# Two transformer blocks on one core: the meta columns moved behind the tokens in the rows of the second block's activations

## What is computed

```python
h = jnp.concatenate([meta, x], axis=1)                  # 16 + 256 rows
hn = rms_norm_2(h, norm_mix_g)
u, gb_in, gc_in, v_in, ga_lin, gbr_lin = jnp.split(hn @ w_in, splits, axis=-1)
pooled = causal_multiscale_pool(u)                       # trailing means over 2, 4, 8, 16 positions
y_a = jnp.einsum("blgc,gcd->blgd", pooled, pool_w) * pool_scale
y_b = (gb_in * causal_depthwise_conv(gc_in * v_in, conv_w)) @ conv_out_w     # 3 taps
h = h + (g_a * y_a + g_b * y_b) @ w_o
...
return rms_norm_2(h, norm_final_g)[:, N_META:]
```

## Time and profile before

| | us |
|---|---|
| median of 3 runs | 2633.67 (2633.49 to 2633.74) |
| the profiled execution | 2633.6 |
| its span in the trace | 2631.8 |
| PE busy | 2620.6 |
| PEld busy | 2558.4 |
| DVE busy | 1572.1 |
| ACT busy | 1172.8 |

### The profile page before, as it was taken

How to read it: one execution, slowest core, us unless ns; L and a number is a source line. 1 busy time by engine, 2 the same in 40 slices (tenths; PEclk the granted TensorE clock), 3 DMA queues, 4 the chain that set the end, 5 groups by cost and what they waited for, 6 DMA issues and landing times.

```text
span 2631.8 us, 50881 instructions
## 1 busy us (share of the span) xinstructions
PE 2620.6 (100%) x21394; PEld 2558.4 (97%) x21394; DVE 1572.1 (60%) x1557; ACT 1172.8 (45%) x1259; POOL 0.8 (0%) x7
## 2 busy tenths in 40 slices
PE   9999999999999999999999999999999999999998
PEld 8989999999999999999999999999999989998997
DVE  6567765555555556795676666556755555555555
ACT  5346544434443444465333333444454434443444
POOL 0000000000000000000000000000000000000000
PEclk9999999999999999999999999999999999999999
DMA  8654655555555565556555555555555555555553
GB/s 294 196 168 145 208 189 192 195 193 192 191 192 193 191 199 194 180 203 199 176 178 189 181 189 180 198 188 199 197 193 192 194 195 191 194 197 194 191 193 128
DMA packets 254275, 503.33 MB, mean 191 GB/s; under 512 B 8130, under 2 KB 11652, under 8 KB 253988
## 3 DMA queue, kind: packets, MB, share of 16 engines
q1 hardware_dynamic: 252180, 497.61, 57.4%
q10 hardware_dynamic: 1952, 3.68, 0.4%
HBM read 498.37 MB, written 2.88 MB: 190 GB/s over the span
## 4 chain that ended last, share of the span: by engine, by line
PE 99%; DMA 0%; DVE 0%; ACT 0%; SPq 0%; issue 0%; DVEq 0%; ACTq 0%
PE ps L1368 49%; PE ps L1379 24%; PE ps L1397 4%; PE ps L1399 4%; PE ps L1398 4%; PE ps L1417 4%; PE ps L1426 4%; PE ps L1421 4%; PE ps L1405 0%; PE ps L1406 0%; PE ps L1407 0%; DMA xtok<-in_x_dram 0%; PE ps L1562 0%; PE ps L1561 0%; PE ps L1560 0%; PE ps L1484 0%
## 5 line engine op out<-in xcount | busy, mean ns | idle before, releaser
L821 DVE TENSOR_TENSOR lo<-raw,hi 128x1024 fp32r<-128x1024 f32 x940 | 1144.5, 1224 | 920.6 <-ACT hi L494 905.7
L494 ACT ACTIVATE hi<-raw 128x1024 fp32r<-128x1024 f32 x940 | 991.6, 1060 | 1243.5 <-PE ps L1379 935.8
L1368 PE MATMUL ps<-A,hi 128*128 128x256 f32 x7283 | 903.6, 277 | 0.0
L1368 PEld LDWEIGHTS ps<-A,hi 128*128 128x128 f32 x7283 | 861.0, 188 | 0.3
L1368 PE MATMUL ps<-B,hi 128*128 128x256 f32 x3962 | 491.3, 277 | 0.0
L1379 PE MATMUL ps<-A,lo 128*128 128x256 f32 x3648 | 488.0, 276 | 0.0
L1368 PEld LDWEIGHTS ps<-B,hi 128*128 128x128 f32 x3962 | 468.1, 188 | 0.1
L1379 PEld LDWEIGHTS ps<-A,lo 128*128 128x128 f32 x3648 | 447.4, 188 | 0.0
L1379 PE MATMUL ps<-B,lo 128*128 128x256 f32 x1984 | 265.3, 276 | 0.0
L1379 PEld LDWEIGHTS ps<-B,lo 128*128 128x128 f32 x1984 | 243.2, 188 | 0.0
L1398 PE MATMUL ps<-lo,B 128*128 128x512 f32 x336 | 130.8, 389 | 0.0
(11 more groups left out here) (243 smaller groups left out, 1196.8 us busy)
## 6 DMA issues: line engine op xcount, KB each, us to landing
raw<-in_w_in_dram SPq DMA_DIRECT2D x136, 1024.0 KB, 5.1
raw<-in_ffn_w_dram SPq DMA_DIRECT2D x132, 1024.0 KB, 5.1
raw<-in_w_gate_up_dram SPq DMA_DIRECT2D x88, 1024.0 KB, 5.0
raw<-in_w_down_dram SPq DMA_DIRECT2D x44, 1024.0 KB, 5.0
raw<-in_w_out_dram SPq DMA_DIRECT2D x16, 1024.0 KB, 5.1
raw<-in_pl_w_gate_dram SPq DMA_DIRECT2D x16, 1024.0 KB, 5.1
raw<-in_conv_out_w_dram SPq DMA_DIRECT2D x16, 1024.0 KB, 5.0
raw<-in_w_o_dram SPq DMA_DIRECT2D x16, 1024.0 KB, 5.0
```

Of the source, the lines that this page charges most:

```text
L494: act.activation(hi[:, slot % RING], raw[:, raw_slot, 2 * (slot % 2):2 * (slot % 2) + 2, :], ACT.Copy).then_inc(hi_ready, 1)
L821: dve.tensor_tensor(lo[:, slot % RING], raw[:, slot // 2 % RAWS, 2 * (slot % 2):2 * (slot % 2) + 2, :], hi[:, slot % RING], ALU.subtract). ...
L1368: pe.matmul(ps[:, b0 + m, 0:T], high(slot, kk, m), x, start=j == 0 and kk == 0 and part == 0, stop=False)
```

## The change

The rows of B are laid out anew for the second block's mixer, and the products of with_meta take other column ranges. In a row of B the tokens' high parts now stand at columns 0 to 255, behind them the last two meta tokens' high parts (256, 257), their low parts (258, 259), the other fourteen's high parts (260 to 273) and low parts (274 to 287); the tokens' low parts stand at 320 to 575. One product of the high pass covers the tokens, the meta tokens' high parts and their low parts; the low-part pass covers the tokens alone; the third pass covers the tokens and the meta tokens' high parts.

```diff
-TOKEN_AT = META + 16
+TOKEN_AT = 16
+LOW_AT = 320
-LO_META = TM + T
+AHEAD_HI, AHEAD_LO, REST_HI, REST_LO = T, T + 2, T + 4, T + 4 + VT0
...
-        B_halves = B[:, :, META:META + 2 * T]
-        B_token = B[:, :, TOKEN_AT:TOKEN_AT + 2 * T]
+        B_high, B_low = B[:, :, 0:T], B[:, :, LOW_AT:LOW_AT + T]
...
                 elif step == "split_meta":
...
-                    given.mark(act.activation(B[:, :, 0:META], metaT[:, :, :], ACT.Copy))
+                    act.activation(B[:, :, AHEAD_HI:AHEAD_HI + 2], metaT[:, :, VT0:META], ACT.Copy)
+                    given.mark(act.activation(B[:, :, REST_HI:REST_HI + VT0], metaT[:, :, 0:VT0], ACT.Copy))
...
                 elif kind == "u2":
                     dve.wait_ge(pieces_used, end)
-                    dve.tensor_tensor(meta_low[:, :, VT0:META], ps[:, b0:b0 + 4, TM:TM + 2], row_of(r_row[:, VT0:META], MT), ALU.mult)
-                    dve.tensor_tensor(meta_low[:, :, 0:VT0], ps[:, b0:b0 + 4, TM + 2:TM + META], row_of(r_row[:, 0:VT0], MT), ALU.mult)
-                    dve.tensor_tensor(win_a[:, :, :], ps[:, b0:b0 + 4, 0:TM], row_of(r_row[:, :], MT), ALU.mult).then_inc(psum_free, 1)
+                    ahead_r, rest_r = row_of(r_row[:, VT0:META], MT), row_of(r_row[:, 0:VT0], MT)
+                    dve.tensor_tensor(meta_low[:, :, VT0:META], ps[:, b0:b0 + 4, AHEAD_LO:AHEAD_LO + 2], ahead_r, ALU.mult)
+                    dve.tensor_tensor(meta_low[:, :, 0:VT0], ps[:, b0:b0 + 4, REST_LO:REST_LO + VT0], rest_r, ALU.mult)
+                    dve.tensor_tensor(win_a[:, :, VT0:META], ps[:, b0:b0 + 4, AHEAD_HI:AHEAD_HI + 2], ahead_r, ALU.mult)
+                    dve.tensor_tensor(win_a[:, :, 0:VT0], ps[:, b0:b0 + 4, REST_HI:REST_HI + VT0], rest_r, ALU.mult)
+                    dve.tensor_tensor(win_a[:, :, META:TM], sums, Rm, ALU.mult).then_inc(psum_free, 1)
...
             def with_meta(seg, g, j, slot, b0, n):
-                ahead = META if seg.reads[1] == "wide" else META - VT0
+                with_lo, with_hi = (REST_LO + VT0, REST_LO) if seg.reads[1] == "wide" else (AHEAD_LO + 2, AHEAD_LO)
...
-                        pe.matmul(ps[:, b0 + m, 0:ahead + T], high(slot, kk, m), B[:, 2 * j + kk, META - ahead:TM],
+                        pe.matmul(ps[:, b0 + m, 0:with_lo], high(slot, kk, m), B[:, 2 * j + kk, 0:with_lo],
...
-                        pe.matmul(ps[:, b0 + m, ahead:ahead + T + ahead], high(slot, kk, m), B[:, 2 * j + kk, TM:TM + T + ahead],
+                        pe.matmul(ps[:, b0 + m, 0:T], high(slot, kk, m), B_low[:, 2 * j + kk, :],
...
-                        last = pe.matmul(ps[:, b0 + m, 0:ahead + T], low(slot, kk, m), B[:, 2 * j + kk, META - ahead:TM],
+                        last = pe.matmul(ps[:, b0 + m, 0:with_hi], low(slot, kk, m), B[:, 2 * j + kk, 0:with_hi],
```

More of the change, by code:

```diff
@@ L252, in bass_two_blocks @@
         ones = sb("ones", [P, P])
+        r_row = sb("r_row", [P, TM])
+        vec2 = sb("vec2", [P, V2N])
         vec1 = sb("vec1", [P, V1K])
@@ L508, in wait_group, with high_parts @@
                 act.nop(nofuse=True)
-            def high_parts(buf, k, a, src, name, n=MT):
+            def high_parts(to, k, src, name, n=MT):
                 for i in range(n):
-                    last = act.activation(buf[:, bass.ds(k + i, 1), a:a + T], src(i), ACT.Copy, scale=gain(name, k + i))
+                    last = act.activation(to[0][:, bass.ds(k + i, 1), :], src(i), ACT.Copy, scale=gain(name, k + i))
                 return last
@@ L563, in evacuate @@
                     more()
-                    given.mark(high_parts(A, k, 0, lambda i: some(h, k + i, 1, 0, T), "ffn" if kind == "res_ffn" else "ffn2"))
+                    given.mark(high_parts(A_parts, k, lambda i: some(h, k + i, 1, 0, T), "ffn" if kind == "res_ffn" else "ffn2"))
                     ready.skip()
@@ L574, in evacuate @@
                     wait_alone(asked)
-                    given.mark(act.activation(some(A if kind == "cb" else to_b, k, 4, 0, T), work[:, :, :], ACT.Copy))
+                    given.mark(act.activation(some((A_parts if kind == "cb" else to_b)[0], k, 4, 0, T), work[:, :, :], ACT.Copy))
                     ready.skip()
@@ L679, in side @@
                     wait(asked)
-                    given.mark(act.activation(some(B_halves, 8 + 4 * c, 4, 0, T), V8[:, 4 * c:4 * c + 4, :], ACT.Copy))
+                    given.mark(act.activation(some(B_high, 8 + 4 * c, 4, 0, T), V8[:, 4 * c:4 * c + 4, :], ACT.Copy))
                     ready.skip()
@@ L746, in side @@
                         for i in range(2):
-                            last = act.activation(B_halves[:, 2 * hd + i, 0:T], ps[:, 6, i * T:(i + 1) * T], ACT.Copy, scale=small[:, 20 + i:21 + i])
+                            last = act.activation(B_high[:, 2 * hd + i, :], ps[:, 6, i * T:(i + 1) * T], ACT.Copy, scale=small[:, 20 + i:21 + i])
                         given.mark(last)
@@ L833, in free_sums, with low_parts @@
                 dve.wait_ge(psum_free, G + 1)
-            def low_parts(buf, k, a, src, name, n=MT):
+            def low_parts(to, k, src, name, n=MT):
                 for i in range(n):
-                    last = dve.scalar_tensor_tensor(out=buf[:, bass.ds(k + i, 1), a + T:a + 2 * T],
-                                                    in0=src(i), scalar=gain(name, k + i), in1=buf[:, bass.ds(k + i, 1), a:a + T],
+                    last = dve.scalar_tensor_tensor(out=to[1][:, bass.ds(k + i, 1), :],
+                                                    in0=src(i), scalar=gain(name, k + i), in1=to[0][:, bass.ds(k + i, 1), :],
                                                     op0=ALU.mult, op1=ALU.subtract)
@@ L969, in evacuate @@
                     more()
[L970 removed]
+                    finish_split(A_parts, k)
                 elif kind == "pool":
@@ L1012, in times_gain, with finish_split @@
                 dve.tensor_tensor(x, x, row_of(gfin_row[:, bass.ds(gi * GC, GC)], 2), ALU.mult)
-            def finish_split(buf, k):
+            def finish_split(to, k):
                 given.skip()
                 wait(given)
-                ready.mark(dve.tensor_tensor(some(buf, k, 4, T, 2 * T), work[:, :, :], some(buf, k, 4, 0, T), ALU.subtract))
+                ready.mark(dve.tensor_tensor(some(to[1], k, 4, 0, T), work[:, :, :], some(to[0], k, 4, 0, T), ALU.subtract))
             def rsqrt(var, mid, r, src, scale, meanwhile=lambda: None):
@@ L1245, in side @@
                         for i in range(2):
-                            last = dve.scalar_tensor_tensor(out=B_halves[:, 2 * hd + i, T:2 * T], in0=ps[:, 6, i * T:(i + 1) * T],
-                                                            scalar=small[:, 20 + i:21 + i], in1=B_halves[:, 2 * hd + i, 0:T],
+                            last = dve.scalar_tensor_tensor(out=B_low[:, 2 * hd + i, :], in0=ps[:, 6, i * T:(i + 1) * T],
+                                                            scalar=small[:, 20 + i:21 + i], in1=B_high[:, 2 * hd + i, :],
                                                             op0=ALU.mult, op1=ALU.subtract)
@@ L1361, in highs @@
                     for part in range(2):
-                        x = X[:, k, at + part * T:at + (part + 1) * T]
+                        x = X[part][:, k, :]
                         for m in range(MT):
@@ L1557, in last_pieces @@
                             k = 2 * j + kk
-                            Xh, Xl = B_token[:, k, a * P:(a + 1) * P], B_token[:, k, T + a * P:T + (a + 1) * P]
+                            Xh, Xl = (x[:, k, a * P:(a + 1) * P] for x in token_parts)
                             to = ps[:, b0 + a, :]
```

41 lines of the change are left out of this document (21 added, 20 removed).

## The result

The changed kernel takes 2638.94 us (median of 18 runs, 2638.69 to 2639.54) where the kernel before takes 2633.76 (18 runs, 2633.49 to 2634.29): **5.2 us more**, a ratio of 1.002 with a 95% interval of 1.0012 to 1.0027. Not one run of the one overlaps one of the other. The forecast was 2631.3 us, the range 2626.5 to 2634.0.

The account below looks back on a forecast made before the run. The prediction took PE's back-to-back products to bound the kernel; gains of 2.1 and 2.6 us less costs of 0.4, 1.7 and 0.2 made -2.4 us against 2633.6, stated as 2631.3 us, range 2626.5 to 2634.0.

Parts of the forecast that it names:

- What bounds the kernel: Whole kernel: time is the sum of PE's product prices; PE is busy 2620.6 of 2631.8 us and waits three times.
- The passes: Convolution and pooled path: columns move between passes, no product added or removed; terms sum to -2.4 us.
- Convolution: Low-part pass 258 to 256 columns gains 2.1 us; high pass 258 to 260 costs 0.4 more; third pass unchanged.
- Pooled path: Low-part pass 272 to 256 gains 2.6 us; high pass to 288 costs 1.7, third pass to 274 costs 0.2.
- the rule of the Trainium skill: Isolated product spacing: columns over 2.4 GHz plus 2.5 ns; convolution would gain nothing, pooled path lose 0.2 us.
- The other engines: DVE's extra small instructions and ACT's split copy of the meta columns stay hidden; costed at nothing.
- Rival 4: Cut product behind the third pass leaves PE dear; some 3260 later 256s cost 4.5 ns more: 2646 us, chance 0.04.
- Rivals 1 and 3: 1: 256s between wide passes stay dear, 2633.8 us, chance 0.14; 3: third pass keeps the cheap state, 2626.6 us, 0.08.
- Rival 2: Wide passes: the 5.5 ns extra comes from operands' start places, so no product pays it afterwards: 2620.5 us, chance 0.08.

Follow-up runs that it names:

- e11: Changed kernel with r_row and vec2 between B and h, so h, ident, ones lie where they lay before and B stays as changed: 2630.63 us.
- e3: Changed kernel with r_row and vec2 put back between A and B: 2676.01 us.
- e4: Kernel before with only r_row and vec2 moved behind ones: 2684.13 us.
- e5: Kernel before with vec2 alone moved behind ones: 2665.05 us.
- e6: Changed kernel with vec2 alone put back between A and B: 2671.40 us.
- e7: Kernel before with rstd_meta (64 bytes) ahead of hi rather than behind lo: 2729.94 us.
- e8: Kernel before with rstd_meta ahead of hi and also r_row and vec2 moved behind ones: 2698.74 us.
- e12: Changed kernel with r_row and vec2 ahead of ident, so ident and ones lie where before but h stays moved: 2636.19 us.
- e13: Kernel before with ln_stats (96 bytes) moved to between B and h: 2639.10 us.
- e14: Kernel before with vec1 (328 bytes) moved to between B and h: 2639.13 us.
- e1: Changed kernel with one product cut in two in the piece behind each of three fp32 side steps: 2631.20 us.
- e15: Kernel before with double_rstd one piece earlier and the second turn of h one piece later, no address changed: 2633.75 us.
- e16: Changed kernel with double_rstd one piece earlier and the second turn of h one piece later, no address changed: 2639.01 us.
- e9: Changed kernel with cuts behind three fp32 side steps, placed one piece later (ga piece 8, f2_up0 pieces 5 and 13): 2631.24 us.
- e10: Kernel before with cuts at ga piece 8 and f2_up0 pieces 5 and 13: 2633.96 us.
- e2: Kernel before with one product cut in two at ga piece 7 and f2_up0 pieces 4 and 12: 2640.01 us.

## Why the prediction was wrong, point by point

**What bounds the kernel** was right: PE's products, one after another, no waits. The whole 5.6 us can be added up from the chain's pieces.

**The passes.** The sum of -2.4 us was mis-sized by little: -2.8 measured (e11 against the kernel before gives -3.1 in all). That it came so near is in part luck, for the two misses, 0.9 us too little gain in the convolution and 0.5 too much in the pooled path, are of opposite sign. By terms:
- Convolution, -2.1 + 0.4 = -1.7 forecast, -2.6 measured. The low-part pass stands at 0.92 where 0.93 was assumed, which makes -2.8 us where -2.1 was forecast; the high pass of 260 did not get dearer by 0.84 ns a product, it costs 0.96 like the 258; the third pass cost 0.2 us more in all (120.2 ns from start to start where it was 119.8).
- Pooled path, -2.6 + 1.7 + 0.2 = -0.7 forecast, -0.2 measured. 288 and 274 columns cost the 1.06 and 1.02 us forecast. The 256 pass is 0.91 in every other piece only and 0.95 between, not 0.91 throughout, so it gained 2.0 and not 2.6: the state behind a 288 alternates.

By the rule of the Trainium skill (TensorE: Matmul & The Clock Gate, section Back-to-back issue gap) the two would have come to 0 and +0.2 us; the trace disagrees, with -2.6 and -0.2.

**The other engines** cost nothing, as forecast: the waits view has no PE wait behind the first block in the changed kernel, and DVE's 1.2 us more are hidden.

**The step that failed** is the sentence "That r_row and vec2 lie elsewhere, and B with them, moves no instruction", with a cost of nothing. It moves no instruction, and it cost 8.4 us. I had found the two states of an ordinary product, and the dear one at 363 and 1921 us, but put its coming down to wide products alone. No wide product stands ahead of those two places: fp32 side steps do. Behind the five at 363, 1180, 1913, 1921 and 1937 us the trace of the kernel before shows the dear state lasting to the next cut twice (363 and 1921) and left within 16 products three times, and I asked neither what brings it there nor what ends it.

**Rival 4** had the mechanism, ordinary products dear over a long stretch, with 4.5 ns each, and its sign. It had the wrong place (the cut behind the wide passes, which lands cheap in the changed kernel: 1.32 us for the 11 products behind it) and the wrong trigger, hence a chance of 0.04. Rivals 1 and 3 fell: the 256 pass is cheaper than its neighbours by more than its columns, and the third pass stayed at 0.96. Rival 2, that the price hangs on where operands start, was wrong for the wide passes (258 columns from the new start still cost 0.96) and right about the kind of cause: e3 to e8 show that the places of the operands change the price of the 256s.

## What to carry to other kernels

In a kernel like this one, where PE streams products of 256 columns back to back, a declaration that moves a buffer can change PE's time: compare the chain's pieces of unchanged lines (16 products at 1.81 or 1.89 us) before crediting or blaming the lines that were edited. Apply a layout change and a product change separately, or put the buffers that were moved where all others keep their places, as e11 does for h, ident and ones: that turned a loss of 5.2 us into a gain of 3.1 and is faster than both kernels.

## What the runs showed of the hardware that I had not expected

- The price of a product of 128x128 weights and 256 columns goes with the distance in SBUF between the weights and the streamed operand, by its remainder by 256 bytes: 113.4 ns at 192 (the kernel before, e8), 119 at 128 (e3, e7), 120 at 0 (e4). Moving 64 bytes from behind lo to ahead of hi cost 96 us of 2634.
- At one and the same distance there are two lasting states, 1.81 and 1.89 us per 16. Which one PE settles in behind a few fp32 products repeats from run to run of a kernel, to judge by its times (2638.69 to 2639.54 over 18 runs). It hangs on where those products' operands lie (e11 to e14), and, at 1921 us, on the state before them (the changed kernel against e1); moving two of the steps by a piece did not change it (e15, e16).
- A cut product can bring either state: out of a settled one, or one that would have lasted, it landed in the cheap one (e9, e10; e1), out of one just falling back in the dear one behind both turns of h, though in the cheap one behind double_rstd (all e2).

Why the distance matters, and what makes a state last, no run here tells: I varied addresses, not the reads themselves. Nor is there a rule that says from the addresses which side step will leave the dear state. Other remainders than multiples of 64 bytes were tried for the side steps alone.
